# Reciprocal roots of eight tiles made by ScalarE as exp(-½ ln) in place of Sqrt and a VectorE reciprocal

## The reference

```
def rms_norm(x, g):
    y = xf * lax.rsqrt(jnp.mean(xf * xf, axis=-1, keepdims=True) + EPS)
    return (y * g.astype(jnp.float32)).astype(x.dtype)
...
for i in range(DEPTH):
    hn = rms_norm(h, g_pre[i])
    ...            # layer 0: gated linear attention; its output is rms_norm(o, g_out) * silu(g), per head
    ...            # layer 1: stick-breaking attention over the K and V that follow layer 0
    h = h + out
    h = ple_add(h, p[i], g_ple[i], ...)      # sigmoid(rms_norm(h, g) @ w_gate) * (p @ w_up)
    if i == N_A - 1:
        k_new, v_new = shared_kv(h, g_kv, w_kv)   # rms_norm(h, g_kv) @ w_kv
return rms_norm(h, g_final), ...
```

## Time and profile before

| | us |
|---|---|
| median of three runs | 1073.97 |
| the three runs | 1070.78, 1073.97, 1078.68 |
| profiled execution, its own time | 1071.41 |
| its span | 1069.7 |
| mean granted TensorE clock | 0.948 of full speed |
| PE busy | 958.0 |
| DVE busy | 644.4 |
| ACT busy | 387.6 |
| POOL busy | 250.0 |

### The profile page before, as it was taken

One profiled execution on the slowest core, in us unless ns is written; L12 is line 12 of the kernel. 1 busy time (PEld: TensorE's weight loads), 2 busy tenths in 40 slices (PEclk: granted clock), 3 DMA queues, 4 the chain that ended last, 5 costly groups with the idle time before them and its releaser, 6 DMA issues.

```text
span 1069.7 us, 14941 instructions
## 1 busy us (share of the span) xinstructions
PE 958.0 (90%) x5257; PEld 651.2 (61%) x5257; DVE 644.4 (60%) x755; ACT 387.6 (36%) x1253; POOL 250.0 (23%) x131
## 2 busy tenths in 40 slices
PE   6889786679988988999987999999999999899995
PEld 3566555557765443444435888788745444499894
DVE  4553216966775788978998272222268677654544
ACT  5302235322322555657453231111233333243323
POOL 2000003463422576556664020000000000011110
PEclk9999888889998999999998999999989999999998
DMA  7978951553333978677898209888866666522202
GB/s 281 329 261 295 371 200 40 165 189 123 124 104 129 364 273 289 229 261 252 322 321 309 70 18 339 286 310 309 311 244 234 239 234 212 182 80 79 79 2 81
DMA packets 111163, 228.27 MB, mean 213 GB/s; under 512 B 7249, under 2 KB 70328, under 8 KB 111088
## 3 DMA queue, kind: packets, MB, share of 16 engines
q1 hardware_dynamic: 53456, 168.46, 44.1%
q10 hardware_dynamic: 57632, 58.86, 16.6%
HBM read 216.18 MB, written 11.11 MB: 212 GB/s over the span
## 4 chain that ended last, share of the span: by engine, by line
PE 51%; DVE 18%; DMA 9%; ACT 6%; issue 5%; POOL 2%; SPq 0%; ACTq 0%; POOLq 0%; DVEq 0%
PE pp L1463 15%; PE pp L1466 7%; PE pp L1851 5%; DVE slot L1149 4%; PE pp L1448 4%; DMA slot<-in_cache_k_dram 4%; PE pp L1810 4%; PE pp L1835 3%; DVE zall L1150 3%; DMA w_raw<-in_gla_w_in_dram 3%; ACT slot L728 2%; POOL slot L552 2%; PE pp L1824 2%; PE pp L1860 1%; DVE rstd L1022 1%
## 5 line engine op out<-in xcount | busy, mean ns | idle before, releaser
L552 POOL TENSOR_TENSOR slot<-slot,qb 128x1024 f32<-128x1024 f32 x80 | 217.6, 2741 | 231.6 <-DMA slot<-in_cache_k_dram 193.4
L994 DVE TENSOR_TENSOR w_lo<-w_raw,w_hi 128x1024 fp32r<-128x1024 f32 x57 | 76.9, 1350 | 107.6 <-ACT w_hi L609 107.6
L1150 DVE TENSOR_REDUCE zall<-slot 128x16 f32<-128x1024 f32 x104 | 125.2, 1216 | 22.2 <-POOL slot L552 20.5
L1466 PE MATMUL pp<-xa_hi,w_hi 128*128 128x512 f32 x200 | 87.0, 435 | 19.4 <-DVE w_lo L994 19.4
L728 ACT ACTIVATE slot<-slot 128x64 f32<-128x64 f32 x384 | 91.8, 241 | 30.8 <-POOL slot L552 30.8
L1451 PE MATMUL pp<-xn,w_unsplit 128*128 128x512 f32 x192 | 86.3, 603 | 4.8 <-DVE q1T L1017 4.8
L1451 PE MATMUL pp<-xn,w_raw 128*128 128x512 f32 x192 | 86.2, 601 | 4.5 <-ACT xn L620 3.7
L609 ACT CAST w_hi<-w_raw 128x1024 fp32r<-128x1024 f32 x58 | 60.4, 1044 | 73.4 <-PE pp L1466 41.2
L1149 DVE TENSOR_TENSOR slot<-slot,qb 128x1024 f32<-128x1024 f32 x48 | 85.1, 1773 | 1.1 <-DMA slot<-in_cache_k_dram 1.1
L1466 PE MATMUL pp<-xa_lo,w_hi 128*128 128x512 f32 x200 | 83.5, 418 | 0.0
L1466 PE MATMUL pp<-xa_hi,w_lo 128*128 128x512 f32 x200 | 82.9, 415 | 0.0
(11 more groups left out here) (278 smaller groups left out, 1670.8 us busy)
## 6 DMA issues: line engine op xcount, KB each, us to landing
slot<-in_cache_k_dram SPq DMA_DIRECT2D x128, 512.0 KB, 5.1
slot<-in_cache_v_dram SPq DMA_DIRECT2D x128, 512.0 KB, 5.4
w_raw<-in_gla_w_in_dram ACTq DMA_DIRECT2D x12, 1024.0 KB, 7.3
slot<-in_gla_w_in_dram SPq DMA_DIRECT2D x24, 512.0 KB, 10.7
w_raw<-in_w_kv_dram ACTq DMA_DIRECT2D x8, 1024.0 KB, 10.6
w_raw<-in_w_ple_gate_dram ACTq DMA_DIRECT2D x6, 1024.0 KB, 5.2
s<-in_state_gla_dram SPq DMA_DIRECT2D x1, 4096.0 KB, 28.9
slot<-in_gla_w_out_dram SPq DMA_DIRECT2D x8, 512.0 KB, 8.0
```

The costliest lines, as they stand in the source:

```text
L552: nc.gpsimd.tensor_tensor(slot[s][:], slot[s][:], qb[:, (n // NPG) % 2, :], ALU.mult).then_inc(S("k_mul_pool"), 1)
L994: nc.vector.tensor_tensor(lo, raw, hi.bitcast(F32), ALU.subtract).then_inc(S("w_split"), 1)
L1150: nc.vector.tensor_reduce(zall[:, n % NPG, b * SH:(b + 1) * SH], at.rearrange("p (h d) -> p h d", d=HD), AX.X, ALU.add).then_inc(S("k_used ...
L1466: last = nc.tensor.matmul(bank[m % 2], w[:, k, :], x[:, 0:NP_TOK], start=(k == 0 and first), stop=(k == KT - 1 and w is wl))
```

## The change

The square root on ScalarE becomes a logarithm, and a second activation behind it raises e to minus half of that, so that ScalarE leaves the reciprocal root itself. VectorE's nine reciprocals of 512 or 520 columns go. The semaphores are renamed with it (`r_root`, `o_root` count the Exp). The Exp waits for the Ln through a semaphore of ScalarE's own (`own.then`). The samples' one-column roots and reciprocals stay.

```diff
@@ rms (ScalarE)
+                t = NP_TOK if i < 2 else T
                 if i < 2:
-                    nc.scalar.activation(rstd[:, 0:NP_TOK], bank[7], ACT.Sqrt, bias=epsc[:], scale=1.0 / D).then_inc(S("r_sqrt"), 1)
+                    own.then(nc.scalar.activation(rstd[:, 0:t], bank[7], ACT.Ln, bias=epsc[:], scale=1.0 / D))
                 else:
-                    nc.scalar.activation(halves(rstd[:]), pp[3][:, :, 0:H2], ACT.Sqrt,
-                                         bias=epsc[:], scale=1.0 / D).then_inc(S("r_sqrt"), 1)
+                    own.then(nc.scalar.activation(halves(rstd[:]), pp[3][:, :, 0:H2], ACT.Ln, bias=epsc[:], scale=1.0 / D))
+                nc.scalar.activation(rstd[:, 0:t], rstd[:, 0:t], ACT.Exp, scale=-0.5).then_inc(S("r_root"), 1)
@@ o_rms (ScalarE)
-                nc.scalar.activation(gkT[:, h, :], bank[4], ACT.Sqrt, bias=epsc[:],
-                                     scale=1.0 / HV).then_inc(S("o_sqrt"), 1)
+                own.then(nc.scalar.activation(gkT[:, h, :], bank[4], ACT.Ln, bias=epsc[:], scale=1.0 / HV))
+                nc.scalar.activation(gkT[:, h, :], gkT[:, h, :], ACT.Exp, scale=-0.5).then_inc(S("o_root"), 1)
@@ recip (VectorE)
-                dve.wait_ge(S("r_sqrt"), i + 1)
-                t = NP_TOK if i < 2 else T
-                own.then(nc.vector.reciprocal(rstd[:, 0:t], rstd[:, 0:t]))
+                dve.wait_ge(S("r_root"), i + 1)
@@ gate_o (VectorE)
-                dve.wait_ge(S("o_sqrt"), h + 1)
+                dve.wait_ge(S("o_root"), h + 1)
                 r = gkT[:, h, :]
-                own.then(nc.vector.reciprocal(r, r))
```

More of the change, by code:

```diff
@@ L1498, in add_squares @@
                 if i and k == 0:
-                    pe.wait_ge(S("r_sqrt"), i)
+                    pe.wait_ge(S("r_root"), i)
                 sq, flags = work[:, n % 2, :], dict(start=(k == 0), stop=(k == KT - 1))
@@ L1668, in gla_scores @@
                 if h >= 2:
-                    pe.wait_ge(S("o_sqrt"), h - 1)
+                    pe.wait_ge(S("o_root"), h - 1)
                 for b in range(TB):
@@ L1779, in sample_scores_back @@
                     pe.wait_ge(S("k_act"), summed_by_act(NPAGES))
-                    pe.wait_ge(S("r_sqrt"), 3)
+                    pe.wait_ge(S("r_root"), 3)
                 if g >= 2:
```

## The result

| | before | changed |
|---|---|---|
| median time (17 runs each) | 1073.97 us | 1067.44 us |
| span of the profiled execution | 1069.7 us | 1064.2 us |
| ratio of the times, 95% interval | | 0.9943 [0.9928, 0.9958] |

A second measurement of the same changed kernel gave 1066.31 us and a ratio of 0.9925 [0.9893, 0.9956]. The prediction said 1067.2 us, between 1063 and 1074, and about the same as before (within 1%). It was right. The change makes nine reciprocal roots in the new way, five norms and four heads, where the title says eight.

The account below looks back on a forecast made before the run. TensorE has the bulk, VectorE paces q1; savings count only where TensorE or a queue feeding it waits for a root. Terms −0.5 −0.2 −0.9 −1.45 −0.97 −1.46 = −5.5 us, from 1072.7 to 1067.2; range 1063 to 1074.

Parts of the forecast that it names:

- The price of one root: At each root, load, Exp and hand-over take 1.94 us in place of 3.38: 1.45 us less for whoever waits.
- Norm 0 and heads 0 and 1: These roots are hidden because VectorE waits for TensorE's products anyway; 0 us.
- Heads 2 and 3: Head 2: earlier copies, capped by TensorE's output matmuls, −0.5 us; head 3: only TensorE's 0.23 us wait can go, −0.2.
- Norm 1: VectorE is free 1.45 us earlier, then waits for GpSimd's later second page: −0.9 us, bounds −1.45 and +1.94.
- Norms 2, 3 and 4: Roots on the path: −1.45 us, −0.97 (the sigmoid's table load now follows the Exp) and −1.46.
- The signs of being wrong: Gap between Ln and load; over 1 us more VectorE wait for GpSimd at norms 1 or 2; g1 not about 3 us earlier.
- theory B: From the experiments: savings ahead of the first gate are given back in attention phases; only norms 3 and 4 gain.
- A switch that costs more than its load: Rival: a switch inside a root costs a second 1.28 us, at four norms; 1072.3 us, chance 0.06.
- Page sums in the place of the wait: Rival at norms 1 and 2: VectorE waits for the late page, +1.94 us each; 1073.5 us, chance 0.10.
- the early phases absorb it: Rival: TensorE or transfers pace ple0 and q1, so norms 1 and 2 give nothing; 1069.6 us, chance 0.08.
- VectorE's whole reciprocal at norm 1: Rival: VectorE gains 3.35 us in place of 0.9, multiplying beside GpSimd in a kinder pattern; 1064.7 us, chance 0.12.
- The rule that was weighed: One table set serves ln and exp, saving 1.3 us more per root, 5.2 over four norms; left out of the sum.

Follow-up runs that it names:

- one table set: Changed kernel with one load of the set holding ln and exp ahead of each root, none between Ln and Exp; 1063.65 us, again 1062.87 us.
- six loads at norm 2: Changed kernel with six more table loads on ScalarE right behind the Exp of norm 2 alone; 1073.66 us, ratio to before 0.9989.
- three more loads: Changed kernel with three more table loads between Ln and Exp at each of norms 1 to 4; 1084.66 us, ratio to before 1.0108.
- two loads more: Changed kernel with two more table loads on ScalarE right behind the Exp of norms 1 and 2; 1072.50 us, ratio to before 0.9994.

## Why the prediction was right, step by step

**The price of one root: right.** Ln 0.69, load 1.28, Exp 0.63 to 0.64, hand-overs 0.02 to 0.03 us. The 1.45 us less per root are 1.48 at norms 2 and 4 (4.16 to 2.68).

**Norm 0 and heads 0 and 1: right as zeros. Heads 2 and 3: right in size, head 3 not in its reason.** Norm 0 alone 1.0007, heads alone 1.0002. From head 0's root to head 2's it is 51.6 or 51.7 us with either kind of root (53.1 in one trace). The −0.7 us for heads 2 and 3 is below what the ratios resolve, and the traces have −0.5 for both together. Head 2's part is real: from its root to head 3's it takes 20.4 us in place of 21.1, in five of the six kernels with the load between Ln and Exp. At head 3 the step was wrong in its reason. The prediction let TensorE's 0.23 us wait cap the saving. In the rows the whole 1.45 us went at VectorE itself, whose four products behind the root took 7.2 to 7.4 us in place of 5.5 to 5.8 beside GpSimd's pages (6.8 in one trace), and with one table set, 1.3 us earlier still, 8.6. From the copy of head 3's output to wo0's first tile it is 18.2 us as before (18.3).

**Norm 1: the place right, the size between its bounds.** The wait for GpSimd at the second page is 0.40 us against a forecast 0.5, GpSimd's wait grew by 1.67 against about 2. From norm 1's root to norm 2's it takes 89.3 us in the mean of five kernels with the reciprocal there (88.9 to 90.5) and 88.3 in the mean of three with Ln and Exp (88.0 to 88.7). That is −1.0 for a forecast −0.9, but with a scatter of its own size. A fourth kernel with Ln and Exp at norm 1, the one with six loads at norm 2, has 87.2, and with it the step is −1.3. The way was not quite the forecast one. VectorE was to be 1.45 us ahead until it met the late page. In the rows its first product behind the root ran beside GpSimd's and took 2.59 us in place of 1.23, which left 0.08 us at norm 1's first tile (8.81 us after the root, 8.89 before), and later products were quicker by as much. The sum had no term for this, so the closeness of −0.9 is in part luck.

**Norms 2, 3 and 4: right.** Root to first dependent tile −1.48, −0.94 and −1.48, against −1.45, −0.97 and −1.46. Each came out the same in every kernel that has the edit there, and with the sign turned in the one with three more loads (+3.86, +3.87, +3.87). Norm 3's is kept: from its root to norm 4's it is 58.8 or 58.9 us in every kernel with Sqrt there and 57.9 with Ln, one load and Exp, which is the forecast −0.97.

**The signs of being wrong.** No gap opened between Ln and load. The start of g1 came 5.8 us earlier, of which 1.8 were there at norm 1's root already. The limit for GpSimd was met at norm 1 (0.4 us more), but over the whole of q1 the changed kernel waits five times 0.4 us for GpSimd's pages, 2.0 us where it was 0.4, and its second trace 1.2. Read for the whole phase, that is past the 1 us of the prediction in one trace of two, and it is one more sign that the pages stand close behind.

**A sentence that did not hold:** that behind norm 2 the page sums may start later, since their pages are used some 14 us after. The 7.7 us held there cost 4.9 us. In the changed kernel itself, where ScalarE is held 1.94 us there, no loss shows: from norm 2's root to the first gate it takes 73.9 and 74.6 us, and 76.6 to 77.8 in the five kernels with Sqrt at that norm. Why this much costs nothing, while two loads more seem to cost 2.4 us in q1, the runs don't settle.

**The sum came out to the tenth by luck.** The stretches around it moved by more than any term, for two reasons that are in the rows and not in the change. First, TensorE's clock. Here is the stretch from VectorE's first `pcum` tile to wo1's first tile (columns as in the earlier trace rows; behind POOL stand the granted clock as a share of full speed, the DMA share and GB/s): before, changed, and with norms 1 and 2 alone changed.

```profile
771.84:942.76 170.92, 163.94 (x898) 84.32 (x891) 117.04 (x213) 60.95 (x125) 0.00 (x0) 0.96 0.62 219
```

```profile
767.00:940.74 173.74, 166.56 (x898) 86.08 (x891) 117.02 (x212) 60.95 (x125) 0.00 (x0) 0.94 0.61 214
```

```profile
770.00:945.76 175.76, 168.78 (x898) 86.80 (x891) 117.03 (x212) 61.04 (x125) 0.00 (x0) 0.93 0.61 212
```

All three have 898 matmuls and 117.0 us on VectorE; TensorE's idle time is 7.0 to 7.2 us in all three. What differs is the granted clock, 0.96, 0.94 and 0.93, and with it the length, 170.9, 173.7 and 175.8 us. With norms 3 and 4 alone changed, where nothing ahead of this stretch differs from before, it is 175.6 us. Over all 14 traces the length follows the clock: 170.9 us at 0.96, 171.8 to 172.6 at 0.95, 173.6 to 174.3 at 0.94, 175.6 and 175.8 at 0.93. So 2.8 of the 3.8 us given back between the first gate and norm 3's root, which had suggested theory B, are the clock of that execution. The kernels with nothing changed ahead of the gate (before, its repetition, norms 3 and 4 alone) take 409.3, 411.8 and 414.0 us there, so the first trace of before is the shortest of them. Behind wo1's first tile, up to the root, it is 49.6 or 49.7 us in every trace. That about 1 us is given back in between is not excluded. The clock is a mean over stretches at 2.4 GHz and shorter ones at the lower level of 1.2. In the changed kernel it is 1.00 from 795 to 920 us and 0.75 over the last 20.7 us, where TensorE is busy for 18.5 of them; before, it was 0.81 over the last 17.8, busy for 15.6. Why it differs between executions these runs don't settle.

Second, GpSimd beside VectorE. The product of a page on VectorE took 1.23 us where GpSimd stood (420.53 in the kernel with loads inside), and 2.59 us where it ran (418.00 beside 414.85 + 4.66 in the changed kernel). So q1's length depends on how the two fall together. VectorE's products from q1's first tile to the first gate (count | busy us, mean ns), before, changed, and one table set:

```profile
L1149 DVE TENSOR_TENSOR slot<-slot,qb 128x1024 f32<-128x1024 f32 x18 | 36.3, 2016 | 0.0
```

```profile
L1148 DVE TENSOR_TENSOR slot<-slot,qb 128x1024 f32<-128x1024 f32 x18 | 32.7, 1819 | 0.0
```

```profile
L1155 DVE TENSOR_TENSOR slot<-slot,qb 128x1024 f32<-128x1024 f32 x18 | 35.7, 1981 | 0.0
```

The changed kernel's profiled execution spends 3.6 us less on them than before and waits 1.6 us more for GpSimd's pages, which makes q1's extra −1.6 us within half a microsecond. Its repetition spends 34.4 us on them. This is in no term of the sum.

Added up from the stretches of several traces and without the clock, the change gives about −0.5 (heads), −3.3 (norm 1's root to the first gate), −1.0 and −1.5 (norms 3 and 4), so −6.3 us, against −6.1 by the ratio. The forecast −5.5 lies within the error of both, and what it lacks is in norms 1 and 2, −2.35 in the sum.

**The rivals.** A switch that costs more than its load falls: no gap at the roots, and 17.7 us for twelve added loads is 1.5 us per load, with 1.28 inside the uncertainty. Page sums in the place of the wait (1073.5) fell for the change, though its mechanism is real once more time is held there. That the early phases absorb it (1069.6) is not ruled out by the ratio of norms 1 and 2 alone (−0.18%, with 0 inside the interval), but by the traces, 163.0 us to the first gate in place of 166.3. VectorE's whole reciprocal at norm 1 (1064.7) can't be excluded by the ratios; the stretch's −1.0 to −1.3 us speaks against it.

**The rule that was weighed** came back another way. The changed kernel has the load between Ln and Exp, as its rows were taken. With one explicit load there is none (501.95 and 502.68 above), and each root reaches the first tile that waits for it 1.28 us sooner, of which the traces show the part at norms 3 and 4 kept. The Trainium skill, "ScalarE: Activation LUTs", section "Table sets: the hidden batching unit", says that one set holds exp and ln, so that one load serves both. This case's trace agrees, once the load names that set; the build's own placement doesn't choose it.

## What to carry to other kernels

Price such a trade at the place, not by engine: VectorE lost 28 us of work and the kernel gained 5 to 8, by the traces nearly all at the four roots that somebody waits for at once. When two functions follow each other, look whether one table set serves both and load it by name ahead of the wait; here that was worth another 3 to 6 us, though at norms 1 and 2 the traces show none of it kept. And a term of 0.1% is confirmed at its place in the trace, in several kernels, since spans and medians carry a clock and a contention that move them by more.

## What the runs showed of the hardware that was not expected

- With the same matmuls and the same idle time, the second attention stretch took 170.9 to 175.8 us from execution to execution, following a granted clock of 0.96 to 0.93.
- A VectorE product of 128x1024 took 1.2 us alone. Of the 38 in the kernel before that ran beside GpSimd's on the same kind of tile for at least a part, 13 took 1.2 us as well and 25 took 1.5 to 3.4, most of them 2.1 to 2.2. At head 3 such an overlap took back the 1.45 us that the root had saved.
- Table loads by name can stand back to back: four took 5.15 us and six 7.72 us, 1.29 us each.
